# Moving products and output transposes between the attention units of block 1

## The reference, cut to what matters

```python
h = rmsnorm(x, g_pre_mix)
proj = h @ w_in
o_a = dsa_attention(...)
o_b = forgetting_attention(...)
o_c = differential_attention(...)
o_d = sliding_window_sink_attention(...)
mix = concatenate([o_a, o_b, o_c, o_d], axis=-1)
x = x + rmsnorm(mix @ w_out, g_post_mix)
```

## Time and profile before

| | |
|---|---|
| median of 3 runs | 2058.63 us |
| lowest and highest | 2057.17 and 2059.23 us |
| the profiled execution | 2057.07 us |
| its span, first to last instruction | 2055.2 us |
| outside the span | 1.87 us |
| TensorE (PE) busy | 1998.4 us, 97% |
| VectorE (DVE) busy | 1567.7 us, 76% |
| ScalarE (ACT) busy | 1206.9 us, 59% |
| mean granted TensorE clock | 0.994 |

### The profile page before, as it was taken

One profiled execution on the slowest core, in us unless ns is written; L12 is line 12 of the kernel. 1 busy time (PEld: TensorE's weight loads), 2 busy tenths in 40 slices (PEclk: granted clock), 3 DMA queues, 4 the chain that ended last, 5 costly groups with the idle time before them and its releaser, 6 DMA issues.

```text
span 2055.2 us, 29975 instructions
## 1 busy us (share of the span) xinstructions
PE 1998.4 (97%) x11564; PEld 1682.5 (82%) x11564; DVE 1567.7 (76%) x1600; ACT 1206.9 (59%) x1281; POOL 97.0 (5%) x162
## 2 busy tenths in 40 slices
PE   7999999998999999999999998999999999999996
PEld 5778888887888889878888887888888888888885
DVE  6777644778764469775547967999999999989998
ACT  5565434556554357444335644777777777777774
POOL 0310000021000000010000000000000000000000
PEclk9999999999999999999999998999999999999998
DMA  8316555532655555155546407999999999999994
GB/s 290 122 60 206 178 184 195 195 129 73 200 183 174 196 191 165 43 171 185 188 158 207 143 2 264 368 352 369 362 366 358 371 363 359 365 364 366 367 360 182
DMA packets 154214, 481.53 MB, mean 234 GB/s; under 512 B 14616, under 2 KB 41728, under 8 KB 153984
## 3 DMA queue, kind: packets, MB, share of 16 engines
q1 hardware_dynamic: 150048, 465.42, 63.6%
q0 software_dynamic: 4064, 14.68, 2.1%
HBM read 477.96 MB, written 2.10 MB: 234 GB/s over the span
## 4 chain that ended last, share of the span: by engine, by line
PE 88%; DVE 8%; ACT 2%; issue 1%; DMA 1%; POOL 0%; SPq 0%; DVEq 0%; ACTq 0%
PE G L658 20%; PE G L660 19%; PE G L659 19%; PE Sp L658 5%; PE Sp L660 5%; PE Sp L659 5%; PE G L685 4%; DVE ring_lo L1979 2%; PE G L654 1%; PE G L649 1%; PE G L650 1%; PE G L1424 1%; DVE ARENA L2429 1%; DVE e_lo L2682 1%; PE G L949 1%
## 5 line engine op out<-in xcount | busy, mean ns | idle before, releaser
L2682 DVE TENSOR_TENSOR e_lo<-e_raw,e_hi 128x1408 fp32r<-128x1408 f32 x384 | 601.2, 1619 | 19.5 <-ACT e_hi L1907 17.3
L1907 ACT ACTIVATE e_hi<-e_raw 128x1408 fp32r<-128x1408 f32 x384 | 523.3, 1380 | 154.3 <-DMA e_raw<-in_moe_w_gate 55.0
L1979 DVE TENSOR_TENSOR ring_lo<-ring,ring_hi 128x2048 fp32r<-128x2048 f32 (+2 forms) x171 | 383.4, 2254 | 188.5 <-ACT ring_hi L1511 187.1
L1511 ACT ACTIVATE ring_hi<-ring 128x2048 fp32r<-128x2048 f32 (+1 forms) x179 | 335.5, 1884 | 235.8 <-PE G L660 201.8
L658 PE MATMUL G<-e_hi,xgTh 128*128 128x512 f32 (+1 forms) x768 | 291.8, 380 | 0.1
L658 PE MATMUL G<-ring_hi,xTh 128*128 128x512 f32 (+2 forms) x736 | 288.8, 392 | 0.0
L660 PE MATMUL G<-e_hi,xgTl 128*128 128x512 f32 (+1 forms) x768 | 288.3, 375 | 0.0
L659 PE MATMUL G<-e_lo,xgTh 128*128 128x512 f32 (+1 forms) x768 | 285.3, 372 | 0.0
L660 PE MATMUL G<-ring_hi,xTl 128*128 128x512 f32 (+2 forms) x736 | 284.2, 386 | 0.0
L659 PE MATMUL G<-ring_lo,xTh 128*128 128x512 f32 (+2 forms) x736 | 283.8, 386 | 0.0
L660 PEld LDWEIGHTS G<-e_hi,xgTl 128*128 128x128 f32 x768 | 144.0, 188 | 25.2
(11 more groups left out here) (410 smaller groups left out, 2897.5 us busy)
## 6 DMA issues: line engine op xcount, KB each, us to landing
e_raw<-in_moe_w_gate SPq DMA_DIRECT2D x128, 704.0 KB, 6.0
e_raw<-in_moe_w_up SPq DMA_DIRECT2D x128, 704.0 KB, 5.9
e_raw<-in_moe_w_down SPq DMA_DIRECT2D x128, 704.0 KB, 5.9
ring<-in_w_in SPq DMA_DIRECT2D x48, 1024.0 KB, 5.0
ring<-in_w_mlp_up SPq DMA_DIRECT2D x32, 1024.0 KB, 5.2
ring<-in_w_mlp_down SPq DMA_DIRECT2D x32, 1024.0 KB, 4.9
ring<-in_w_out SPq DMA_DIRECT2D x16, 1024.0 KB, 4.9
ring<-in_ffn_w_gate SPq DMA_DIRECT2D x22, 512.0 KB, 3.9
```

What stands on the lines that cost most here:

```text
L1511: nc.scalar.activation(ring_hi[:, n % H, 0:m], ring[:, n % R, 0:m], ACT.Copy).then_inc(w_hi.sem, 1)
L1907: nc.scalar.activation(e_hi[:, u, :], e_raw[:, u, :], ACT.Copy).then_inc(w_hi.sem, 1)
L1979: v.tensor_tensor(ring_lo[:, n % R, cs], ring[:, n % R, cs], ring_hi[:, n % H, cs].bitcast(F32), ALU.subtract).then_inc(w_lo.sem, 1)
L2682: v.tensor_tensor(e_lo[:, u, :], e_raw[:, u, :], e_hi[:, u, :].bitcast(F32), ALU.subtract).then_inc(w_lo.sem, 1)
```

## The change

The input columns of token block 1 that come from tiles j = 2 and 3 (332 wide) are cut by contraction tiles k. Tile 2 was done whole behind `values(2)`; now two of its k go ahead of the loop over the units, two between `logits(2)` and `values(0)`. Tile 3 was done whole behind `output_transposes(0, 1)`; now two of its k go between `logits(4)` and `values(2)`, one behind the transposes of the C heads of block 1, one behind those of the D heads. `out_rows(1, 0)` goes ahead of `output_transposes(0, 0)` in unit 5. Three waits for `T[0]` that stand alone are dropped. Every matmul and transpose stays.

```diff
-            def last_columns(j, tb):
+            def last_columns(j, tb, ks=range(4)):
...
-                for k in range(4):
+                for k in ks:
...
-                if tb:
+                if tb and ks[-1] == 3:
                     last.then_inc(w_used.sem, 1)
-                elif j % 2:
+                elif j % 2 and not tb:
                     last.then_inc(in_half.sem, 1)
...
             last_columns(1, 1)
             bank_free_t(1)
+            last_columns(2, 1, range(2))
             for u in range(NU):
                 tb = UNITS[u][2]
                 prob_transposes(u, 0)
                 if u + 2 < NU:
                     logits(u + 2)
+                if u == 0:
+                    last_columns(2, 1, range(2, 4))
+                if u == 2:
+                    last_columns(3, 1, range(2))
                 if tb:
                     prob_transposes(u, 1)
                 if u == 5:
+                    out_rows(1, 0)
                     output_transposes(0, 0)
-                    out_rows(1, 0)
                 if u in (6, 7):
-                    if u == 6:
-                        bank_free_t(0)
                     out_rows(2, 0, range(2 * (u - 6), 2 * (u - 5)))
...
                 values(u)
                 if u == 2:
-                    last_columns(2, 1)
                     rotated_transposes(QK_C, 1, c_rotated)
-                    bank_free_t(0)
+                    last_columns(3, 1, range(2, 3))
                 if u == 3:
                     rotated_transposes(QK_D, 1, d_rotated)
+                    last_columns(3, 1, range(3, 4))
                     output_transposes(0, 1)
-                    last_columns(3, 1)
                 if u == 4:
                     pe.wait_ge(g_act.sem, G_ACT * l + 2 * IN_N)
-                    bank_free_t(0)
                     out_rows(0, 0)
```

## The result

The changed kernel takes 2064.51 us (median of 7 runs, 2064.20 to 2066.66) against 2057.59 us for the kernel before (7 runs, 2057.02 to 2059.23). The ratio is 1.0033, with a 95% interval of [1.0023, 1.0043]: slower by 6.9 us, where no change was forecast. The profiled execution took 2064.44 us, its span 2062.6 us.

What follows compares the result with a forecast made beforehand. The prediction took TensorE's stream, busy 97% of the span, as the bound. Gains and losses left 0.18 us per layer, twice 0.36: median 2058.63 to 2058.3, called no change (0.85), range 2055.0 to 2062.0.

Steps and rivals of the forecast that it cites:

- The walk through the waits: Reckoning of layer 0's start times at full clock, place by place, doubled for layer 1; gain 0.18 us per layer.
- The new wait ahead of unit 4: Behind unit 3's output transposes: TensorE idle some 2.9 us, released by VectorE's low part; sign 2.5 to 3 us.
- that ahead of values(5): In unit 5: a new stall of 1.5 to 1.9 us ahead of values(5), released by VectorE's low part.
- The wait ahead of unit 7's second transposes: In unit 7: a wait of 0.3 to 0.4 us ahead of the second transposes, given as a sign.
- The sum of the waits: Sign for the whole stage: TensorE's waits stay near 5.5 us per layer; under 3.5 would show the forecast wrong.
- the sum's 0.36 us: Net gain over both layers: 0.18 us per layer, twice 0.36, taking the median from 2058.63 to 2058.3.
- The rival: Clock falls in the gap 116.5 to 119.35 ahead of unit 4's transposes: 3.1 to 13.5 us slower; chance 0.08.
- seven shorter stalls: Layer 0's TensorE stalls of 0.69 to 1.06 us, 5.71 together; the clock stayed full through stalls up to 1.06.
- the loss of unit 5 stays: Unit 5's 0.40 us not won back: 0.8 to 2 us slower, 2059.4 to 2060.6; part of the forecast, no separate chance.
- the cheapest case: Lowest price of the clock's fall in the gap ahead of unit 4: 3.1 us for two layers, time 2061.4.
- all seven stalls vanish: Whole stage: with slack on VectorE and ScalarE all 11.4 us are won, 2047.2; chance 0.07.
- unit 6 gave it back: Unit 6: lone wait dropped, output rows 0.38 behind the transposes; gain 0.96, from 0.40 behind to 0.56 ahead.

Runs made afterwards that it cites:

- The filled kernel: Changed kernel plus 20 useless matmuls 256 wide behind unit 3's output transposes: 2057.73 us, ratio 0.9996 to the kernel before.
- tile 3 back: Changed kernel with tile 3's twelve products whole behind unit 3's output transposes again, other moves kept: 2058.45 us, ratio 1.0001 to the kernel before.
- both undone: Changed kernel with tile 3 whole behind the output transposes and unit 5 in the old order: 2056.66 us, ratio 0.9994 to the kernel before.
- logits(6) alone in the gap: Changed kernel with unit 5 in the old order and logits(6) moved ahead of unit 4's transposes: 2056.85 us, ratio 0.9990 to the kernel before.

## Why the prediction was wrong

**The walk through the waits was right.** Taking off the 1.26 us of the start: unit 4's transposes came at 119.38 (forecast 119.35), unit 3's at 111.37 (111.43), output transposes of half 1 at 116.06 (116.10). The new wait ahead of unit 4 was 2.69 us (forecast some 2.9, 2.5 to 3 as the sign), released by VectorE's low part, and that ahead of values(5) 1.48 (1.5 to 1.9 as the sign). The wait ahead of unit 7's second transposes was 0.22 (0.3 to 0.4). The sum of the waits stayed at 5.6 us per layer (5.5). VectorE was the full engine that frees `T[0]`, and took back what the moves had won. The filled kernel measures this part by itself: 0.9996 of the kernel before, where the sum's 0.36 us would be 0.9998, and 0.56 us in its trace.

**The step that failed is the clock, which the sum puts at nothing and the rivals at a chance of 0.08.** The rival named the place, the mechanism and a price of 3.1 to 13.5 us with 8 as the value. The runs show some 3.0 us per layer: values(5) came at 136.91 - 1.26 = 135.65, and the walk at full clock has it at 132.63. Twice 3.0 less the walk's 0.36 is 5.7, near the 5.5 that the trace has for both layers; the 7.4 of the two spans are these 5.5, the 1.26 of the start and the 0.65 of later stages. How the 6.9 between the medians divides was not measured, since the other runs have no trace. What was wrong was the argument against the rival: that the clock had stayed full through stalls up to 1.06 on this stage. The forecast itself had a gap of 2.9 us, 2.7 times longer, with four transposes ahead of it, and no row showed such a gap at full clock.

The prediction also says that the trace shows such a fall only in the routing. The kernel before shows a second one, behind its last matmul (2040.87): the granted clock is 1.00 up to 2042, 0.80 over 2042 to 2045 and 0.50 from there to the end. It costs nothing there, but it shows the clock going down within 4 us of the last work. These two places deserved more weight than seven shorter stalls.

The rule of the Trainium skill ("TensorE: Matmul & The Clock Gate", section "Why this matters for your kernels"), that an idle gap between bursts of matmuls throws the clock to half, was cited for that rival. The traces agree that this happens, here behind 2.69 us, in every layer profiled of the two kernels that have that gap. They differ on the size: 2.69 us, and 1.57 where tile 3 alone was moved, are shorter gaps than the section warns of, and the measurement decides.

**The range** ended at 2062.0, built from the loss of unit 5 staying and the spread; of the clock's price it held only the cheapest case (2061.4). **The other rivals** (all seven stalls vanish; the loss of unit 5 stays) did not happen; unit 5's loss, alone, was 0.60 us per layer as reckoned, and in the changed kernel unit 6 gave it back.

**What stays open.** What decides a fall in a sparse stretch where waits of about 1 us stand near each other: three kernels (tile 3 back, both undone, logits(6) alone in the gap) had it in layer 1 and not in layer 0, with nearly the same waits ahead of it in both. How often these fall is known only roughly, from the mean granted clock of the runs; the place is seen only in the profiled executions. Also open is why the half clock of the routing lasted some 3 us longer in one execution than in the other.

## What to carry to other kernels

When products are moved to fill small stalls, look at the place they leave: if it has a wait behind it, several short stalls become one long one, and the sum of the waits says nothing of that. Price every gap that a change opens on TensorE with half clock behind it, and read the granted clock in windows of a few us around it; a busy share does not show it. Put work into such a gap that hangs on nothing in flight (here the scores two units ahead), and leave some products for the longest wait in place of spreading them evenly.

## What the runs showed of the hardware

The kernel got faster when TensorE was given 40 matmuls without use: from 2064.51 us (ratio 1.0033) to 2057.73 (0.9996).

The length of a wait alone does not decide a fall. A wait of 1.57 us behind a wait of 0.32 and four transposes was followed by one in both layers. A wait of 1.58 behind products 512 wide was not (the kernel before at 2039.20, granted clock 1.00 from 2036 to 2042), and neither was one of 1.48 with output rows and four transposes ahead of it. A fall also came among matmuls 32 and 64 wide with no wait above 0.38. These are single places, and they do not separate what stands around a wait from chance.

At half clock the scores of the same form took 2.51 in place of 1.47 us, and not double. The stretches at half lasted about 3, 7 and 10 us in different executions of much the same stage.
